# The scaling of attention probabilities moves from VectorE to GpSimd, and with it the copies around the transposes

## The reference

```python
# kind a, 4 heads with two maps each (differential attention)
logits = einsum(q, k) * scale + bias;  p = softmax(logits)
attn = p[:, :, 0] - lam * p[:, :, 1];  o = attn @ v
# kind b, 8 heads: window of 128 keys, one extra "sink" logit in the softmax
p = softmax(concat([logits, sink]))[..., :-1];  o = p @ v
# kind c, 8 heads: at 256 rows there is one block, so a plain causal softmax
p = softmax(logits);  o = p @ v
mix = ga * (ya @ w_oa) + gb * (yb @ w_ob) + gc * (yc @ w_oc)
```

## Time and profile before

| | |
|---|---|
| three runs | 2637.99, 2640.82, 2640.91 us; median 2640.82 |
| profiled execution | 2637.99 us, its span in the trace 2636.2 us |
| attention loop on TensorE | from 190.03 to 234.61 us of the span |
| TensorE, VectorE, ScalarE, GpSimd busy over the span | 94%, 57%, 47%, 7% |

### The profile page before, as it was taken

One profiled execution on the slowest core, in us unless ns is written; L12 is line 12 of the kernel. 1 busy time (PEld: TensorE's weight loads), 2 busy tenths in 40 slices (PEclk: granted clock), 3 DMA queues, 4 the chain that ended last, 5 costly groups with the idle time before them and its releaser, 6 DMA issues.

```text
span 2636.2 us, 38986 instructions
## 1 busy us (share of the span) xinstructions
PE 2484.2 (94%) x15976; PEld 2064.9 (78%) x15976; DVE 1510.8 (57%) x1964; ACT 1250.1 (47%) x1654; POOL 191.6 (7%) x210
## 2 busy tenths in 40 slices
PE   8999999999999999999999999998999998777797
PEld 6887888877788888888887888777788887676775
DVE  4457544675665666655445444455665655666666
ACT  5446444564555555554444445443444454444443
POOL 2002000000000000000001000000000011333320
PEclk9999999999999999999999999999999999889998
DMA  8756666655555555547555655444656684122252
GB/s 247 242 170 139 207 206 209 210 176 191 187 172 183 191 179 181 178 163 254 192 192 176 201 190 169 135 144 160 218 173 216 215 263 153 48 67 68 78 192 96
DMA packets 242408, 463.41 MB, mean 176 GB/s; under 512 B 9952, under 2 KB 39849, under 8 KB 240480
## 3 DMA queue, kind: packets, MB, share of 16 engines
q1 hardware_dynamic: 223488, 422.08, 48.3%
q0 software_dynamic: 18464, 39.22, 5.4%
q10 hardware_dynamic: 320, 0.13, 0.0%
HBM read 446.66 MB, written 14.74 MB: 175 GB/s over the span
## 4 chain that ended last, share of the span: by engine, by line
PE 46%; DVE 5%; ACT 3%; issue 2%; ACTq 0%; DVEq 0%
PE bank L324 13%; PE bank L326 13%; PE bank L325 12%; PE bank L2067 2%; PE bank L1894 1%; PE bank L1916 1%; DVE d_products L2037 1%; PE bank L2159 1%; PE bank L2450 1%; PE bank L2132 0%; DVE d_minus_b L2006 0%; PE bank L1559 0%; ACT w_high L255 0%; DVE d_t L1981 0%; PE bank L1900 0%
## 5 line engine op out<-in xcount | busy, mean ns | idle before, releaser
L261 DVE TENSOR_TENSOR w_low<-raw,w_high 128x1024 fp32r<-128x1024 f32 x768 | 932.1, 1225 | 832.4 <-ACT w_high L255 831.3
L255 ACT ACTIVATE w_high<-raw 128x1024 fp32r<-128x1024 f32 x768 | 805.0, 1057 | 953.2 <-PE bank L326 933.7
L324 PE MATMUL bank<-w_high,b_h_high 128*128 128x512 f32 x704 | 278.3, 395 | 8.7 <-DVE w_low L261 7.2
L326 PE MATMUL bank<-w_high,b_h_low 128*128 128x512 f32 x704 | 275.1, 391 | 0.0
L325 PE MATMUL bank<-w_low,b_h_high 128*128 128x512 f32 x704 | 275.0, 391 | 0.0
L324 PE MATMUL bank<-w_high,a_h_high 128*128 128x512 f32 (+1 forms) x640 | 247.8, 387 | 2.3 <-DVE w_low L261 2.3
L326 PE MATMUL bank<-w_high,a_h_low 128*128 128x512 f32 (+1 forms) x640 | 246.7, 385 | 0.0
L325 PE MATMUL bank<-w_low,a_h_high 128*128 128x512 f32 (+1 forms) x640 | 246.6, 385 | 0.0
L324 PE MATMUL bank<-w_high,d_high 128*128 128x512 f32 x512 | 203.1, 397 | 10.6 <-DVE d_low L2573 10.6
L324 PE MATMUL bank<-w_high,c_x_high 128*128 128x512 f32 x512 | 203.3, 397 | 0.6 <-DVE c_x_low L465 0.6
L325 PE MATMUL bank<-w_low,d_high 128*128 128x512 f32 x512 | 201.5, 393 | 0.0
(11 more groups left out here) (366 smaller groups left out, 3679.1 us busy)
## 6 DMA issues: line engine op xcount, KB each, us to landing
raw<-in_w_up SPq DMA_DIRECT2D x88, 1024.0 KB, 5.1
raw<-in_w_in SPq DMA_DIRECT2D x76, 1024.0 KB, 5.1
raw<-in_ev_w_in SPq DMA_DIRECT2D x48, 1024.0 KB, 5.1
raw<-in_w_down SPq DMA_DIRECT2D x44, 1024.0 KB, 5.0
raw<-in_w_out SPq DMA_DIRECT2D x16, 1024.0 KB, 5.0
raw<-in_ev_w_out SPq DMA_DIRECT2D x16, 1024.0 KB, 5.0
raw<-in_od_w_r SPq DMA_DIRECT2D x16, 1024.0 KB, 5.0
raw<-in_od_w_k SPq DMA_DIRECT2D x16, 1024.0 KB, 5.0
```

The lines of the kernel that those rows point to most:

```text
L255: act.activation(wh[n % 4][:, :, 0:width], raw_half, ACT.Copy).then_inc(sem("w_high_made"), 1)
L261: vec.tensor_tensor(wl[n % 4][:, :, 0:width], raw_half, wh[n % 4][:, :, 0:width].bitcast(F32), ALU.subtract).then_inc(sem("w_low_made"), 1)
L324: pe.matmul(b, xh, wh[n][:, k % 2, 0:width], start=(c == 0 and k == 0), stop=False)
L326: mm = pe.matmul(b, xl, wh[n][:, k % 2, 0:width], start=False, stop=(c == j.chunks - 1 and k == 3))
```

## The change

GpSimd gets the scaling. It waits for a new semaphore, `sums_inverted`, after VectorE's reciprocals, and its order becomes load, scale, load, scale: heads 8 to 11 are loaded one ahead of each of scale(0) to scale(3), heads 12 to 19 two ahead of each of scale(4) to scale(7). VectorE keeps the joining, now at the end of its iteration. ScalarE's copy L860 stays for kind a alone; VectorE copies both turned banks for b and c. The copy of the kind-a result moves from ScalarE to VectorE. The first gate-bias load on GpSimd waits for all twelve results, and a few waits on TensorE change their semaphore.

```diff
+        def scale(i):
+            gp.wait_ge(sem("sums_inverted"), i + 1)
+            for u in (1,) if HP[i].kind == "a" else (0, 1):
+                for t, c, w in TILES:
+                    p = PR[i % 3][u][:, c:c + w]
+                    op = gp.tensor_scalar(p, p, small[:, sums_at(i, u, t)], None, ALU.mult)
+            op.then_inc(sem("probs_scaled"), 1)
...
-        for h in range(8, 20):
-            load_bias(h)
+        for i in range(NP):
+            if i < 4:
+                load_bias(8 + i)
+            elif i < 8:
+                load_bias(4 + 2 * i)
+                load_bias(5 + 2 * i)
+            scale(i)
...
-        gp.wait_ge(sem("y_made"), 8)
+        gp.wait_ge(sem("y_made"), NP)
...
-                pe.wait_ge(sem("probs_scaled"), i - 3)
+                pe.wait_ge(sem("probs_scaled"), i + 1)
...
-            if i >= 5:
-                pe.wait_ge(sem("second_probs_turned"), i - 4)
...
-            if i >= 4:
-                pe.wait_ge(sem("second_probs_turned"), i - 3)
             if i >= 2:
-                pe.wait_ge(sem("y_rows_made" if i < 6 else "y_made"), i - 1 if i < 6 else i - 5)
+                pe.wait_ge(sem("y_made"), i - 1)
...
-            if 2 <= i < NP + 2:
+            if 2 <= i and i - 2 < NP and HP[i - 2].kind == "a":
                 act.wait_ge(sem("probs_transposed"), i - 1)
...
                 act.activation(PT[i % 2][0][:, :], PS[0][:, 0:384], ACT.Copy).then_inc(sem("probs_turned"), 1)
...
-                if HP[n].kind == "a":
-                    act.activation(YR[:, :, 128 * n:128 * n + 128], bank[:, c:c + 256].rearrange("p (t e) -> p t e", t=2),
-                                   ACT.Copy).then_inc(sem("y_rows_made"), 1)
...
-                for u in (1,) if HP[n].kind == "a" else (0, 1):
-                    for t, c, w in TILES:
-                        p = PR[n % 3][u][:, c:c + w]
-                        op = vec.tensor_scalar(p, p, small[:, sums_at(n, u, t)], None, ALU.mult)
...
+                    vec.reciprocal(sums, sums).then_inc(sem("sums_inverted"), 1)
...
-                if n >= 6:
+                if n >= 2:
                     vec.wait_ge(sem("values"), n - 1)
-                vec.tensor_copy(PT[n % 2][1][:, :], PS[1][:, 0:384]).then_inc(sem("second_probs_turned"), 1)
+                for u in range(2):
+                    op = vec.tensor_copy(PT[n % 2][u][:, :], PS[u][:, 0:384])
+                op.then_inc(sem("probs_turned"), 1)
...
+                if b == 0:
+                    vec.wait_ge(sem("values"), n + 1)
+                    vec.tensor_copy(YR[:, :, 128 * n:128 * n + 128], bank[:, c:c + 256].rearrange("p (t e) -> p t e", t=2)
+                                    ).then_inc(sem("y_made"), 1)
...
+            if 1 <= i <= NP and HP[i - 1].kind == "a":
+                n = i - 1
+                vec.wait_ge(sem("probs_scaled"), n + 1)
+                for t, c, w in TILES:
+                    p = PR[n % 3][0][:, c:c + w]
+                    op = vec.scalar_tensor_tensor(out=p, in0=p, scalar=small[:, sums_at(n, 0, t)],
+                                                  in1=PR[n % 3][1][:, c:c + w], op0=ALU.mult, op1=ALU.add)
+                op.then_inc(sem("maps_joined"), 1)
```

More of the change, by code:

```diff
@@ L862, in a_act @@
                 exps(i)
-            if i >= 3:
+            if i >= 3 and HP[i - 3].kind != "a":
                 n = i - 3
@@ L866, in a_act @@
                 act.wait_ge(sem("values"), n + 1)
-                if HP[n].kind == "a":
-                    act.activation(YR[:, :, 128 * n:128 * n + 128], bank[:, c:c + 256].rearrange("p (t e) -> p t e", t=2),
-                                   ACT.Copy).then_inc(sem("y_rows_made"), 1)
-                else:
-                    act.activation(YH[1 if HP[n].kind == "b" else 2][:, n % 4, :], bank[:, c:c + 256], ACT.Copy
-                                   ).then_inc(sem("y_high"), 1)
+                act.activation(YH[1 if HP[n].kind == "b" else 2][:, n % 4, :], bank[:, c:c + 256], ACT.Copy
+                               ).then_inc(sem("y_high"), 1)
             if i == NP:
@@ L875, in a_act @@
                     for t in range(2):
-                        act.wait_ge(sem("y_rows_made"), h + 1)
+                        act.wait_ge(sem("y_made"), h + 1)
                         n = 2 * h + t
@@ L981, in a_vec @@
                 sums = small[:, 64 + 4 * n:68 + 4 * n]
-                vec.reciprocal(sums, sums).then_inc(sem("a_vec"), 1)
-                nv += 1
-                vec.wait_ge(sem("a_vec"), nv)
                 if HP[n].kind == "a":
-                    vec.tensor_scalar(small[:, 66 + 4 * n:68 + 4 * n], small[:, 66 + 4 * n:68 + 4 * n], small[:, 37:38],
-                                      None, ALU.mult).then_inc(sem("a_vec"), 1)
+                    vec.reciprocal(sums, sums).then_inc(sem("a_vec"), 1)
                     nv += 1
                     vec.wait_ge(sem("a_vec"), nv)
-                for u in (1,) if HP[n].kind == "a" else (0, 1):
-                    for t, c, w in TILES:
-                        p = PR[n % 3][u][:, c:c + w]
-                        op = vec.tensor_scalar(p, p, small[:, sums_at(n, u, t)], None, ALU.mult)
[L994 to L1002, removed]
+                    vec.tensor_scalar(small[:, 66 + 4 * n:68 + 4 * n], small[:, 66 + 4 * n:68 + 4 * n], small[:, 37:38],
+                                      None, ALU.mult).then_inc(sem("sums_inverted"), 1)
                 else:
-                    op.then_inc(sem("probs_scaled"), 1)
+                    vec.reciprocal(sums, sums).then_inc(sem("sums_inverted"), 1)
             if 2 <= i < NP + 2 and HP[i - 2].kind != "a":
@@ L1007, in a_vec @@
                 vec.wait_ge(sem("probs_transposed"), n + 1)
-                if n >= 6:
+                if n >= 2:
                     vec.wait_ge(sem("values"), n - 1)
-                vec.tensor_copy(PT[n % 2][1][:, :], PS[1][:, 0:384]).then_inc(sem("second_probs_turned"), 1)
-            if i >= 3 and HP[i - 3].kind != "a":
+                for u in range(2):
+                    op = vec.tensor_copy(PT[n % 2][u][:, :], PS[u][:, 0:384])
+                op.then_inc(sem("probs_turned"), 1)
+            if i >= 3:
                 n = i - 3
@@ L1014, in a_vec @@
                 b = "abc".index(HP[n].kind)
-                vec.wait_ge(sem("y_high"), n - 3)
-                vec.tensor_tensor(YL[b][:, n % 4, :], bank[:, c:c + 256], YH[b][:, n % 4, :].bitcast(F32), ALU.subtract
-                                  ).then_inc(sem("y_made"), 1)
+                if b == 0:
+                    vec.wait_ge(sem("values"), n + 1)
+                    vec.tensor_copy(YR[:, :, 128 * n:128 * n + 128], bank[:, c:c + 256].rearrange("p (t e) -> p t e", t=2)
+                                    ).then_inc(sem("y_made"), 1)
+                else:
+                    vec.wait_ge(sem("y_high"), n - 3)
+                    vec.tensor_tensor(YL[b][:, n % 4, :], bank[:, c:c + 256], YH[b][:, n % 4, :].bitcast(F32), ALU.subtract
+                                      ).then_inc(sem("y_made"), 1)
+            if 1 <= i <= NP and HP[i - 1].kind == "a":
[6 more added lines that the diff above has]
+                op.then_inc(sem("maps_joined"), 1)
         vec.wait_ge(sem("squares_made"), 2)
```

## The result

The changed kernel took 2661.85 us (median; 2653.30 to 2665.07 in 4 runs) beside 2640.86 us for the kernel before: 21 us slower, a ratio of 1.0076 with a 95% interval of 1.0049 to 1.0102. Two later sets of the same kernel gave ratios of 1.0087 (1.0061 to 1.0113) and 1.0066 (1.0048 to 1.0084). The forecast was +5.0 us, in a range up to 2650.7; the direction was right and the size was not.

What follows compares the result with a forecast made beforehand. VectorE's 3.54 us an iteration sets the loop's pace, TensorE's 3.37 next; GpSimd becomes the bound for pairs 4 to 7. Delay of 5.8 less 0.8 regained gives +5.0 us: 2645.8 us against the median, range 2641.0 to 2650.7.

Steps and rivals of the forecast that it cites:

- The pace, and what lies behind the loop: Attention loop: VectorE's 3.54 us an iteration against TensorE's 3.37; the 165.39 us behind it absorb no early or late start.
- the lower end of the range: Whole kernel's time: 2641.0 us, from S = 1.20 less half the spread of the runs.
- What the scaling costs on GpSimd: GpSimd in the loop: four scalings take 1.65 us, halfway between copy and spread operand; bounds 1.20 to 2.35.
- S: Length of four scaling instructions on GpSimd, taken as 1.65 us; a kind-a pair has half, 0.83.
- rule of 7 us for one of S: Loop's sum moves with S: 1.75 in kind a, 4 in the middle, 1.2 in the drain.
- Kind a: Pairs 0 to 3: the scaling's trip to GpSimd and back, about 1.0 us, adds 0.4 us an iteration.
- Pairs 4 to 7: Loads queue before scalings, GpSimd becomes the bound: 4.48 us an iteration against 3.54; pair 7's transposes start 5.8 us later.
- The way out: Pairs 8 to 11 to the loop's end, 16.05 us before: 0.8 us comes back, with 0 and 1.5 as ends.
- Loads in time, gate-bias load, ScalarE at nothing: Loop and just behind: bias loads land before use, the later gate-bias load and ScalarE's lost work cost nothing.
- the slower one: GpSimd multiplies at a two-input rate, shown at scale(4) to scale(7): +5.3 to +9.9 us; chance 0.42.
- The first-use cost: At scale(0) GpSimd stops once to fetch code for a new operation; +11 by the skill's 6 us; chance 0.04.

Runs made afterwards that it cites:

- loads_act: Changed kernel with the bias loads of heads 8 to 19 issued from ScalarE's queue instead of GpSimd's; 2650.33 us, ratio to before 1.0035.
- late: Changed kernel with GpSimd scaling only pairs 8 to 11, without loads in front, VectorE the others; 2647.11 us beside 2643.61 before, ratio 1.0007.
- mid: Changed kernel with GpSimd scaling only pairs 4 to 7, four loads ahead of each, VectorE the others; 2650.63 us beside 2640.07 before, ratio 1.0037.
- prices kernel: Kernel with the scaling put back on VectorE, plus 60 operations on idle GpSimd ahead of the loop; ran once for its rows, 2644.78 us.
- filled: Changed kernel with 99 identity transposes added on TensorE where it waits for GpSimd; two sets, 2659.42 and 2656.29 us beside 2643.61 and 2640.07 before.
- scalar_copies: Kernel before with VectorE's copy of the second turned bank given to ScalarE; 2643.50 us beside 2640.07 before, ratio 1.0011.

## Why the prediction was wrong

- **The pace, and what lies behind the loop**: right. 15.8 of the 16.5 us between the profiled executions are in the loop, and TensorE is busy for the whole 165.39 us behind it. Two slips in the sums bear on nothing: VectorE's terms add up to 3.47 us (its copy takes 0.54 where a wait follows it) for the row's 3.54, and the lower end of the range comes to 2641.3 rather than 2641.0.
- **What the scaling costs on GpSimd**: this is the step that failed. The prediction took S = 1.65 us for four scalings, with 2.35 as the upper end "by a two-input operation with nothing in its way". Measured: 2.98, outside the range. An operation with one streamed input was taken to lie between a copy (0.83 ns a column) and a two-input product (2.13); it costs 2.50, more than either. The rows were read rightly, but none was of this operation, and nothing in them bounds it from above. By the prediction's own rule of 7 us for one of S the loop's sum would have been 5.0 + 7 x 1.33 = 14.3 us; without clock falls the runs showed 14.4. So the way from S to the time held, and its starting value did not.
- **Kind a**: mechanism right, size off by the same S. scale(3) started at 206.70 instead of 205.6; that is 0.8 us an iteration where the prediction had 0.4, and by its own sum 1.50 us on GpSimd would have made it 1.1. The 14.3 is near in part because small errors offset each other: up to pair 7's transposes the rule gives 13.5 us where 13.3 were measured, and on the way out 0.8 where 1.1 were.
- **Pairs 4 to 7**: right as a mechanism (loads and scalings in series, GpSimd the bound), shown by loads_act, late and mid. The round was 5.86 us for 4.48, and pair 7's transposes came at 231.71 for 224.4.
- **The way out**: 0.8 us was to come back. In the third profile of the changed kernel the stretch from pair 7's transposes (231.33) to the end (248.46) took 17.13 us, 1.1 more than the 16.05 before, since S is in it too, and in the first (231.71 to 250.28) 18.57, 1.4 more again by the clock.
- **Loads in time, gate-bias load, ScalarE at nothing**: right. No scores waited for a load, and nothing waited for the gate bias behind the loop.
- **The clock**: the prediction had no term for it. TensorE's longer and more frequent waits brought falls of the granted clock, worth 0 to 1.4 us in the changed kernel's profiles and 2.8 in mid's; the kernel before, with one wait of 1.90 us near its end, had none in its profile.
- **The rivals**: the slower one came true and beyond its end. The first-use cost did not: the first TENSOR_SCALAR starts at 195.27, 0.1 us after VectorE's factor (194.94 and 0.23 us long). GpSimd had been idle for 1.89 us there, which could hide something; in the prices kernel nothing can, and the first starts at 70.53, 0.1 us behind a MEMSET (69.55 and 0.88 us long).
- **Left open**: the times differ by more than the loops. By the means of its three sets the changed kernel is 18.8, 21.2 and 17.2 us above the kernel before, and the loops profiled in these sets are 15.8, 14.9 and 14.4 us longer: 3 to 6 us remain. The profiled executions took 2654.84, 2654.14 and 2650.34 us, near or at the lowest of their sets, so the traces show the kernel at its fastest. The two filled sets are 15.5 and 16.8 above, for loops 14.4 longer. The clock in the slower executions may cost more than the 1.4 us seen, but side by side, on one chip, filling gained 0.4 us by the means. Where the rest lies is not shown.

## What to carry to other kernels

Work given to an idle engine has three prices: its length there, what already stands in that engine's queue with no one waiting for it, and the handovers; the second became a bound here as soon as TensorE waited for something behind it. In this kernel the price of an operation on GpSimd wasn't bounded by the rows of other operations, not even by heavier ones: measure the operation itself before it decides a range. And where the next engine's work is close behind, relief gives little: VectorE's 3.54 us an iteration could only fall to TensorE's 3.37.

## What the runs showed of the hardware

- On GpSimd a TENSOR_SCALAR on float32 costs 2.50 ns a column, with a column or a constant as scalar, and the same product as TENSOR_TENSOR with a spread column 1.67; 256 columns take 0.93 and 0.61 us. In the Trainium skill, "GPSIMD Engine Reference", section 4.1 calls one-input operations roughly line-rate: the copies here agree (0.83 ns a column), TENSOR_SCALAR doesn't.
- TensorE at its lower level takes 1.54 to 1.66 us for groups of matmuls that take 0.87 to 0.98; it fell there behind waits of 2.74 and 1.86 us in the changed kernel, 2.79 and 2.44 in mid and 1.84 in scalar_copies. It didn't behind one of 2.42 in the changed kernel and of 1.90 in the kernel before, nor in the three profiles where filler transposes stood in the waits.
- ScalarE's queue took 0.37 to 0.49 us to issue one of the bias loads that take GpSimd 0.73 (23 of 24 in loads_act; one took 1.50).
- In the prices kernel each GpSimd operation that started while VectorE made `w_low` (1.23 us, from `raw` and `w_high`) ended later by what that had left, less some 0.15 us: 1.77 us for 0.93 in one row. Those already under way weren't lengthened.
